# Prompt attention: scaling after the value products, rotary queries by a table, alternating score banks

## The reference

```python
q = jnp.einsum('btr,rhd->bthd', rmsnorm(cq, prm['g_q']), prm['w_q_up'])
q_nope = q[..., :QK_NOPE]                     # 64 wide
q_pe = rope(q[..., QK_NOPE:], q_pos)          # 32 wide
kpe = rope(kpe_raw, q_pos)
...
s = (jnp.einsum('bthn,bshn->bhts', q_nope[:, q0:q1], k_nope[:, :q1])
     + jnp.einsum('bthp,bsp->bhts', q_pe[:, q0:q1], kpe[:, :q1]))
s = s.astype(jnp.float32) * SCALE
s = jnp.where(causal, s, NEG_INF)
pr = jax.nn.softmax(s, axis=-1).astype(v.dtype)
outs.append(jnp.einsum('bhts,bshv->bthv', pr, v[:, :q1]))
```

## Time and profile before

| | |
|---|---|
| three runs | 2546.79, 2549.93, 2551.59 us; median 2549.93 |
| profiled execution | span 2552.2 us from the first to the last instruction; no other time of it is given |
| PE busy | 2334.8 us, 91% |
| DVE, ACT, POOL busy | 1276.2, 616.9, 389.0 us |
| the four pairs | 1011.2 to 1345.2 us |

### The profile page before, as it was taken

How to read it: one execution, slowest core, us unless ns; L and a number is a source line. 1 busy time by engine, 2 the same in 40 slices (tenths; PEclk the granted TensorE clock), 3 DMA queues, 4 the chain that set the end, 5 groups by cost and what they waited for, 6 DMA issues and landing times.

```text
span 2552.2 us, 36828 instructions
## 1 busy us (share of the span) xinstructions
PE 2334.8 (91%) x14466; PEld 2153.4 (84%) x14466; DVE 1276.2 (50%) x1891; ACT 616.9 (24%) x977; POOL 389.0 (15%) x249
## 2 busy tenths in 40 slices
PE   4999999999999998788877879899999999999896
PEld 3999999999999997445444559899999999999895
DVE  7333333333336544887788865533333333334746
ACT  4111111111113132333332342311111111112423
POOL 0000000000000000999999000000000000000000
PEclk9999999999999999788888989999999999999998
DMA  4111111111110113100014520111111111111201
GB/s 138 34 42 41 49 42 40 49 49 49 48 43 30 51 36 47 17 13 13 0 45 118 144 67 17 50 50 50 44 47 41 41 41 49 41 41 50 68 24 68
DMA packets 53229, 123.01 MB, mean 48 GB/s; under 512 B 9889, under 2 KB 29778, under 8 KB 52962
## 3 DMA queue, kind: packets, MB, share of 16 engines
q1 hardware_dynamic: 47826, 113.02, 15.3%
q10 hardware_dynamic: 4032, 4.13, 0.6%
q0 software_dynamic: 1296, 4.82, 0.6%
HBM read 115.85 MB, written 6.09 MB: 48 GB/s over the span
## 4 chain that ended last, share of the span: by engine, by line
PE 70%; DVE 15%; issue 6%; ACT 6%; DMA 1%; SPq 1%; ACTq 0%; DVEq 0%; POOL 0%; POOLq 0%
PE ps L412 21%; PE ps L414 20%; PE ps L413 20%; PE ps L579 3%; DVE red L1128 2%; DVE cacc L1439 2%; DVE n L1142 2%; PE ps L604 1%; ACT whi L795 1%; PE ps L594 1%; DVE prod L1170 1%; DVE wlo L1120 1%; DVE h L1160 1%; ACT pr L977 1%; DVE n_lo L1149 1%
## 5 line engine op out<-in xcount | busy, mean ns | idle before, releaser
L412 PE MATMUL ps<-n_hi,wlo 128*128 128x352 f32 x2832 | 925.8, 327 | 13.1 <-DVE n_lo L1530 4.6
L414 PE MATMUL ps<-n_hi,whi 128*128 128x352 f32 x2832 | 915.4, 323 | 0.0
L413 PE MATMUL ps<-n_lo,whi 128*128 128x352 f32 x2832 | 914.3, 323 | 0.0
L412 PEld LDWEIGHTS ps<-n_hi,wlo 128*128 128x128 f32 x2832 | 536.4, 189 | 18.5 <-issue 6.5
L413 PEld LDWEIGHTS ps<-n_lo,whi 128*128 128x128 f32 x2832 | 537.8, 190 | 2.4 <-issue 1.0
L414 PEld LDWEIGHTS ps<-n_hi,whi 128*128 128x128 f32 x2832 | 537.0, 190 | 0.0
L1170 DVE TENSOR_TENSOR prod<-gact,ps 128x352 f32<-128x352 f32 x132 | 68.7, 521 | 731.8 <-ACT gact L828 731.8
L412 PE MATMUL ps<-hid_hi,wlo 128*128 128x352 f32 x1104 | 365.3, 331 | 26.6 <-DVE h L1160 13.8
L414 PE MATMUL ps<-hid_hi,whi 128*128 128x352 f32 x1104 | 358.0, 324 | 0.0
L413 PE MATMUL ps<-hid_lo,whi 128*128 128x352 f32 x1104 | 357.6, 324 | 0.0
L828 ACT ACTIVATE gact<-ps 128x352 f32<-128x352 f32 x132 | 61.3, 464 | 1128.8 <-PE ps L414 1128.8
(11 more groups left out here) (167 smaller groups left out, 1827.5 us busy)
## 6 DMA issues: line engine op xcount, KB each, us to landing
raw<-in_wstream SPq DMA_DIRECT2D x167, 512.0 KB, 3.6
ctile<-in_cache SPq DMA_DIRECT2D x100, 144.0 KB, 2.4
h<-in_xT SPq DMA_DIRECT2D x3, 1408.0 KB, 10.9
out_yT<-n POOLq DMA_DIRECT2D x3, 1408.0 KB, 5.9
ctile<-in_cache ACTq DMA_DIRECT2D x28, 144.0 KB, 2.8
pw<-in_pairw SPq DMA_DIRECT2D x4, 800.0 KB, 4.4
out_ckvT<-ckv SPq DMA_DIRECT2D x1, 1056.0 KB, 9.0
cs<-in_trig SPq DMA_DIRECT2D x1, 528.0 KB, 5.3
```

Source lines behind the costliest of these rows:

```text
L412: nc.tensor.matmul(out, w_l, x_h, start=first, stop=False)
L413: nc.tensor.matmul(out, w_h, x_l, start=False, stop=False)
L414: return nc.tensor.matmul(out, w_h, x_h, start=False, stop=last)
```

## The change

- Probabilities stay raw exponentials. Row sums of all blocks and heads of a pair go to `psums`; at the pair's end one reciprocal gives `precs`, 16 products of `precs` (each a column spread over 64) with the identity lay the reciprocals over the output's layout in banks 0 and 1 (`reciprocals`), DVE multiplies `at_raw` by them, ACT takes the high part of all 1024 columns, DVE the low part. `transposes(i)` wait for the exponential (`s_free`) instead of `p_norm`.
- The query weights get 128 columns per head: 64 plain, 32 rotary, the same 32 with halves swapped. `z` 0 to 5 are now two heads times three row blocks. DVE copies each out with one instruction that multiplies by SCALE and a table `tab` of ones, cos and sin rows. The keys hold the rotated shared key twice (rows 64 to 95 and 96 to 127), so the products of the scores add the two halves. The sample queries get the same sum by one product with a stacked identity each.
- For blocks 0 to 3 a head's scores alternate between its two banks (`sbase`); `scores(0)` and `scores(1)` are issued ahead of the loop and `scores(i+2)` from block i on, up to scores 3. From scores 4 on it is as before.
- ACT does the exponentials of block i before the copies of block i-1's transposes. All six taps of DVE stand behind its six copies of the queries.
- Loads: `cs` 264 KB instead of 528, `tab` 528 KB more, the weights of a pair 896 KB instead of 800. SP's load of the second cache tile waits for the last query copy instead of the rotation.

The diff, cut to its core:

```diff
@@ -259,6 +263,10 @@
     def rows(r):
         return slice(r * RB, (r + 1) * RB)
+    def sbase(i, hh):
+
+        return 1024 * hh + (512 * (i % 2) if i < 4 else 0)
+
     def kap(i):
         return i if i < 4 else 4 + 2 * (i - 4)
...
-            for z in range(3):
+            for z in range(6):
+                hh, r = divmod(z, NRB)
                 if z == 2:
-                    pe.wait_ge(av_lo, QB * p + 2)
-                pe.wait_ge(proj_free, Z_PROJ * p + (z + 1))
-                proj(z, 2 * ROPE, RB, QC, PW_PE, 2 * ROPE, lambda c: cq[:, c, rows(z)]).then_inc(proj_ready, 1)
-            for z in range(3, 6):
-                pe.wait_ge(proj_free, Z_PROJ * p + (z + 1))
-                proj(z, P, RB, QC, PW_NOPE, P, lambda c: cq[:, c, rows(z - 3)]).then_inc(proj_ready, 1)
+                    pe.wait_ge(av_out, QB * p + 2)
+                if z < 4:
+                    pe.wait_ge(proj_free, 6 * p + (3 + z))
+                else:
+                    pe.wait_ge(q_free, 6 * p + (z - 3))
+                proj(z, P, RB, QC, PW_Q + hh * QC * P, P, lambda c: cq[:, c, rows(r)]).then_inc(proj_ready, 1)
             for z in range(6, 8):
-                pe.wait_ge(proj_free, Z_PROJ * p + (z + 1))
+                pe.wait_ge(q_free, 6 * p + (z - 3))
...
-            pe.wait_ge(rope_done, p + 1)
+                nc.tensor.matmul(ps[0:ROPE, 4 + z % 4, C96 * NEW:(C96 + 1) * NEW], ident[NOPE:P, P:P + ROPE],
+                                 q[NOPE:P, z - 10, SEQ:ROWS], start=True, stop=True).then_inc(proj_ready, 1)
             pe.wait_ge(kpe_ready, 1)
+            pe.wait_ge(kpe_twice, 1)
...
             def scores(i):
                 for hh in range(2):
-                    pe.wait_ge(s_free, 2 * QB * p + (2 * i + hh + 1))
+                    pe.wait_ge(s_free, 2 * QB * p + (2 * (0 if i < 2 else i - 1 if i < 4 else i) + hh + 1))
                     w = (i + 1) * P
+                    s0 = sbase(i, hh)
                     for c in range(0, w, 512):
                         e = min(w, c + 512)
-                        last = nc.tensor.matmul(psf[:, hh * 1024 + c:hh * 1024 + e], q[:, hh, i * P:(i + 1) * P],
+                        last = nc.tensor.matmul(psf[:, s0 + c:s0 + e], q[:, hh, i * P:(i + 1) * P],
                                                 k[:, hh, c:e], start=True, stop=True)
                     last.then_inc(s_ready, 1)
...
-                    pe.wait_ge(p_norm, 2 * QB * p + (2 * i + hh + 1))
+                    pe.wait_ge(s_free, 2 * QB * p + (2 * i + hh + 3))
...
+            def reciprocals():
+
+                pe.wait_ge(rec_ready, p + 1)
+                for i in range(QB):
+                    for hh in range(2):
+                        last = nc.tensor.matmul(ps[VH * hh:VH * (hh + 1), i // 4, i % 4 * P:(i % 4 + 1) * P],
+                                                precs[:, 2 * i + hh:2 * i + hh + 1].broadcast_to([P, VH]),
+                                                ident[:, 0:P], start=True, stop=True)
+                last.then_inc(bc_ready, 1)
+
+            pe.wait_ge(at_scaled, p + 1)
             scores(0)
-            pe.wait_ge(proj_free, Z_PROJ * p + (4 + Z_PROJ))
+            scores(1)
+            pe.wait_ge(proj_free, 6 * p + 12)
             for i in range(QB):
-                if i + 1 < QB:
+                if i + 2 < 4:
+                    scores(i + 2)
+                elif 4 <= i + 1 < QB:
                     scores(i + 1)
                 if i:
                     values(i - 1)
                 transposes(i)
             values(QB - 1)
+            reciprocals()
...
+        pe.wait_ge(at_scaled, PAIRS + 1)
...
                 act.wait_ge(av_ready, QB * p + (i + 1))
-                nc.scalar.activation(n_hi[:, p, i * P:(i + 1) * P], ps[:, 6 + i % 2, 0:P], ACT.Copy).then_inc(av_hi, 1)
+                nc.scalar.activation(at_raw[:, p, i * P:(i + 1) * P], ps[:, 6 + i % 2, 0:P], ACT.Copy).then_inc(av_out, 1)
             for i in range(QB):
-                if i:
-                    untile(i - 1)
                 for hh in range(2):
                     u = 2 * i + hh
                     act.wait_ge(s_max, 2 * QB * p + (u + 1))
+                    if i >= 2:
+                        act.wait_ge(t5_ready, 12 * p + (kap(i - 2) + (1 if i < 6 else 2)))
                     w = (i + 1) * P
-                    nc.scalar.activation(pr[:, i % 2, hh, 0:w], psf[:, 1024 * hh:1024 * hh + w], ACT.Exp,
+                    s0 = sbase(i, hh)
+                    nc.scalar.activation(pr[:, i % 2, hh, 0:w], psf[:, s0:s0 + w], ACT.Exp,
                                          bias=stat[:, 4 + u % 4:5 + u % 4],
-                                         accum_out=stat[:, 8 + u % 4:9 + u % 4]).then_inc(s_free, 1)
+                                         accum_out=psums[:, u:u + 1])\
+                        .then_inc(s_free, 1)
+                if i:
+                    untile(i - 1)
                 if i >= 2:
-                    high_av(i - 2)
+                    take_av(i - 2)
             untile(QB - 1)
-            high_av(QB - 2)
-            high_av(QB - 1)
+            take_av(QB - 2)
+            take_av(QB - 1)
+            act.wait_ge(at_scaled, p + 2)
+            nc.scalar.activation(n_hi[:, p, 0:SEQ], at_raw[:, p, 0:SEQ], ACT.Copy).then_inc(av_hi, 1)
...
+            for z in range(6):
+                hh, r = divmod(z, NRB)
+                ve.wait_ge(proj_ready, Z_PROJ * p + (z + 1))
+                nc.vector.scalar_tensor_tensor(out=q[:, hh, rows(r)], in0=ps[:, 4 + z % 4, 0:RB], scalar=SCALE,
+                                               in1=tab[:, rows(r)], op0=ALU.mult, op1=ALU.mult).then_inc(q_free, 1)
             pair_taps(0, PAIR_TAPS)
-
-            ve.wait_ge(proj_free, Z_PROJ * p + (4 + 3))
-            nc.vector.memset(stat[:, 22:23], 0.0)
-            step.hit(nc.vector.stream_shuffle(qsw[:, :], qraw[:, :], swap))
-            step.sync()
-            step.hit(nc.vector.tensor_tensor(qraw[:, :], qraw[:, :], cs[:, 0, :], ALU.mult))
-            step.hit(nc.vector.tensor_tensor(qsw[:, :], qsw[:, :], cs[:, 1, :], ALU.mult))
-            step.sync()
-            nc.vector.tensor_tensor(q[NOPE:NOPE + ROPE, 0, :], qraw[0:ROPE, :], qsw[0:ROPE, :], ALU.add)
-            nc.vector.tensor_tensor(q[NOPE:NOPE + ROPE, 1, :], qraw[ROPE:2 * ROPE, :], qsw[ROPE:2 * ROPE, :],
-                                    ALU.add).then_inc(rope_done, 1)
-            ve.wait_ge(rope_done, p + 1)
-            for hh in range(2):
-                step.hit(nc.vector.tensor_copy(qabs[NOPE:K96, 2, :, bass.ds(8 * p + 4 * hh, 4)],
-                                               q[NOPE:NOPE + ROPE, hh, SEQ:ROWS].rearrange("p (b t) -> p b t", b=DEC_B)))
...
-                    diag = psf[:, 1024 * hh + i * P:1024 * hh + (i + 1) * P]
+                    s0 = sbase(i, hh)
+                    diag = psf[:, s0 + i * P:s0 + (i + 1) * P]
                     step.hit(nc.vector.tensor_tensor(diag, diag, tri[:, :], ALU.add))
                     step.sync()
-                    nc.vector.reduce_max(stat[:, 4 + u % 4:5 + u % 4], psf[:, 1024 * hh:1024 * hh + (i + 1) * P], AX.X,
+                    nc.vector.reduce_max(stat[:, 4 + u % 4:5 + u % 4], psf[:, s0:s0 + (i + 1) * P], AX.X,
                                          negate=True).then_inc(s_max, 1)
                 if i:
                     untile(i - 1)
-                for hh in range(2):
-                    u = 2 * i + hh
-                    ve.wait_ge(s_free, 2 * QB * p + (2 + u + 1))
-                    step.hit(nc.vector.reciprocal(stat[:, 12 + u % 4:13 + u % 4], stat[:, 8 + u % 4:9 + u % 4]))
-                    step.sync()
-                    w = (i + 1) * P
-                    nc.vector.tensor_scalar(pr[:, i % 2, hh, 0:w], pr[:, i % 2, hh, 0:w],
-                                            stat[:, 12 + u % 4:13 + u % 4], None, ALU.mult).then_inc(p_norm, 1)
-                if i >= 2:
-                    low_av(i - 2)
             untile(QB - 1)
-            low_av(QB - 2)
-            low_av(QB - 1)
+            ve.wait_ge(s_free, 2 * QB * p + (2 + 2 * QB))
+            nc.vector.reciprocal(precs[:, :], psums[:, :]).then_inc(rec_ready, 1)
+            ve.wait_ge(bc_ready, p + 1)
+            ve.wait_ge(av_out, QB * p + (2 + QB))
+            nc.vector.tensor_tensor(at_raw[:, p, 0:SEQ].rearrange("p (a n) -> p a n", a=2),
+                                    at_raw[:, p, 0:SEQ].rearrange("p (a n) -> p a n", a=2), ps[:, 0:2, :], ALU.mult)\
+                .then_inc(at_scaled, 1)
+            ve.wait_ge(av_hi, p + 1)
+            nc.vector.tensor_tensor(n_lo[:, p, 0:SEQ], at_raw[:, p, 0:SEQ], n_hi[:, p, 0:SEQ].bitcast(f32),
+                                    ALU.subtract).then_inc(av_lo, 1)
```

More of the change, by code:

```diff
@@ L939, in evac @@
                 for d, s in dsts:
[L940 removed]
+                    last = nc.scalar.activation(d, s, ACT.Copy)
                 last.then_inc(proj_free, 1)
[L943 to L947 removed]
```

111 lines of the change are left out of this document (57 added, 54 removed).

## The result

| | before | after |
|---|---|---|
| median of 4 runs, us | 2550.03 (2546.79 to 2551.59) | 2500.67 (2499.17 to 2503.64) |
| profiled span, us | 2552.2 | 2497.0 |
| loop over four pairs, first projection to its end, us | 334.0 | 280.5 |
| loop's end to the layer norm's sums, us | 141.5 | 143.1 |

After to before is 0.9815, 95% interval 0.9801 to 0.9828: 49 us faster, where I had forecast 23.

A forecast was written before the change was run, and what follows sets the result against it. PE was taken to bound the kernel, losing time to waits and 1.2 GHz stretches. Projections to first add -0.1, first add to next projections -30.3, after the loop +4.0 and +3.4: -23.0, so 2527 us, range 2503 to 2549.

The forecast's parts named there:

- First add: Start of each pair: first triangle add on DVE 24.6 us after the projections start, behind six taps.
- Blocks 4 to 7: Later blocks of each pair: 29.6 us in all, where pair 3 had 32.4.
- the price of the level: Loop over pairs: two second stretches at 1.2 GHz left in, +14.9 us, from the excess of pairs 0 and 1 over pair 3.
- the first blocks: First triangle add to the end of transposes 3 in each pair: 15 us, with 1.2 GHz expected behind PE's first wait.
- the 20.3: Time in us that pair 3 needed before the change from first triangle add to the end of transposes 3.
- pair 0 and the stretch ahead: Pair 0's start: weights land 1.3 us later, first triangle add at 1039.7, 2.6 us earlier than before.
- the tail: After the last pair: ACT's cache loads and first copies wait for reciprocals, multiply and copy, +4.0 us.
- The cover by POOL: Sample attention starts some 26 us earlier, so three more slow tiles run beside POOL's taps: +3.4 us.
- rival B: Loop over pairs: PE's clock stays up with denser work, 2501 to 2512 us; chance 0.25.
- B's second stretch: Later part of a pair: no pair has a second stretch at 1.2 GHz, -14.9 us.
- its 11 us for the first one: First blocks of four pairs: at best the first 1.2 GHz stretch is gone too, four times 15 - 12.3, -11 us.
- The start: Projections to first triangle add over the four pairs: -2.6 - 0.1 + 2.4 + 0.2 = -0.1 us.

## Why the prediction was right in sign and wrong in size

*Right.* First add 24.4 to 25.2 us after the projections (24.6 forecast). PE's idle ahead of scores 2 is 4.5 to 5.2 us in pairs 1 to 3 (4.5). Blocks 4 to 7 take 28.8 to 30.5 us (29.6), reciprocals 1.9 (2.0), the wait between the heads' transposes 1.0 to 1.2 (about 1), none of weight ahead of the scores.

*Wrong: the price of the level, 14.9 us.* The step that failed is "The wait that I leave between transposes keeps PE thin, so I leave two such stretches: +14.9". Two pairs have one, 2 and 3, but it holds one group of values, 3.23 and 3.26 us for 1.75: 3.0 us together. The stretches of before, from which I took the price, held scores 6 and part of scores 7. With the short ones in them, blocks 4 to 7 took 118.7 us over the four pairs; I had given them 118.4 and the 14.9. The run with ACT's old order has waits of 1.46 us ahead of the scores and 1.2 GHz in scores 7 of every pair; the runs with the order changed and the scaling gone have waits of 1.0 to 1.5 us between the transposes, scores at once behind them, and 2.4 GHz in scores 4 to 7 of every pair. Longer waits there, 2.55 to 3.62 us with the scaling left in, go with 1.2 GHz again. So the two parts took the low level out of these scores. Why a wait of 1.46 us goes with either level, and values 6 are low in two pairs of four behind the same wait of 0.83, stays open. From the last values to the next scores PE now spends 2.6 us (1.31 us of products end at 1196.75, scores 7 start at 1199.36) where the old order had 3.6 (1211.37 to 1214.98). I had read the size of the new wait from the chain rightly and still carried the old price over.

*Wrong: the first blocks, 5 us, and their reason.* They took 12.1, 15.0, 13.8 and 14.2 us where I gave 15 each; pair 0, with scores 2 and 3 at 1.56 and 1.88, is at the 12.3 that I had for the full level. And I had put the gain over the 20.3 down to the alternate banks; without them the four pairs' first blocks are 4.3 us longer and the loop is no longer than after. Most of it comes from the exponentials, which no longer stand behind copies and need no scaling: these two parts alone bring the 87.7 us of before down to 65.0.

*Wrong: pair 0 and the stretch ahead, 4.4 us.* Pair 0's first add came at 1034.31, not 1039.7. Its weights were waited for 8.6 us in place of 7.6 (forecast +1.3), but behind a stage that had ended 2.4 us earlier in this execution, so the projections began at 1009.87; they and the last copy took 13.3 us in place of 14.2, and the six taps 11.2 in place of 13.0. The other three pairs together were 1.0 later than forecast.

*Wrong: the tail, 5.8 us.* I counted the last pair's reciprocals twice, 2.0 us, in the pair and again behind it. The sample attention's copies then came 7.2 us after the loop's end in place of 8.0, since PE's first latents lie under the multiply and ACT's issues; I had +2.0. The cover by POOL was right in kind, and near in size: +2.4, as what is left over of the stretch, for +3.4. It is small because before paid most of it already: the 40 small taps of DVE take 25.8 us there and 28.4 after, where 9.7 are left without POOL's last taps.

The other 2.0 us lie in the rest of the program, where nothing was changed; single executions differ by as much.

That the time is at the lower end of rival B is in part luck. B's second stretch nearly holds (14.6 of 14.9 us in blocks 4 to 7), but of its 11 us for the first one only 5 came: with 2.93 us for scores 2 in pairs 1 and 3, the low level behind the first wait is still there. The start and the tail, which B shared with the forecast, made up for it.

## What to carry to other kernels

A loop over three engines that is closed by the order on one of them gains little from taking work off another alone (here 11 us, and 41 with the order changed as well); find the queue in which the awaited instruction stands behind one that nobody awaits yet. Price a PE stage at both clock levels, with the waits as they will be after the change, and treat the level as part of the forecast, not as a remainder. And look for the next bound before it shows: here the taps ahead of each pair's first add, one copy's place and DVE's work beside the sample attention were worth 38 us more.

## What I had not expected of the hardware

Rows of zeros in a contraction made a kernel faster, by 0.41% (0.25 to 0.58), and products that nobody reads by 0.66% (0.44 to 0.88), with the granted clock over the span at 0.967 and 0.969 against 0.957 in the profile before. Where a low stretch falls moved with each of these edits: filled at the pair's start it came at scores 2 and 3, with 128 rows at scores 7. Why it comes at just these places, and why the width of a product bears on it, stays open.
